# State-space output products in pairs of banks with the latents' norms ahead of them, and split latent-attention scores, in a one-core Trainium2 block kernel

## What is computed

```python
z = x @ w_in                      # x: layer-normed input
xs, gs, cq, ckv, kr, gm = split(z)
# state-space branch, 32 groups of 16 channels, 64 complex states
y = einsum(c_re, h_re) - einsum(c_im, h_im) + d_skip * xs
y = gelu(y);  y = y * sigmoid(y @ w_glu + b_glu)
# latent attention, 4 heads, 128 + 64 rotary dimensions
q  = rms_norm(cq) @ w_uq;   kv = rms_norm(ckv) @ w_ukv
s  = (q_nope @ k_nope.T + rot(q_rope) @ rot(k_rope).T) * scale   # causal
o  = softmax(s) @ v
mix = concat(ys * silu(gs), o * silu(gm)) @ w_out
u   = ALPHA * x + mix
```

## Time and profile before

| | us |
|---|---|
| median of 3 runs (2264.51 to 2267.73) | 2265.94 |
| the profiled execution's own time | 2264.39 |
| its span, first to last instruction | 2262.4 |
| TensorE busy / ACT / DVE / POOL | 2186.6 / 753.0 / 1163.2 / 1190.1 |
| mean granted TensorE clock | 0.991 |

### The profile page before, as it was taken

One profiled execution on the slowest core, in us unless ns is written; L12 is line 12 of the kernel. 1 busy time (PEld: TensorE's weight loads), 2 busy tenths in 40 slices (PEclk: granted clock), 3 DMA queues, 4 the chain that ended last, 5 costly groups with the idle time before them and its releaser, 6 DMA issues.

```text
span 2262.4 us, 27546 instructions
## 1 busy us (share of the span) xinstructions
PE 2186.6 (97%) x10904; PEld 1606.9 (71%) x10904; DVE 1163.2 (51%) x1479; ACT 753.0 (33%) x1163; POOL 1190.1 (53%) x808
## 2 busy tenths in 40 slices
PE   8999999999998999999999999998999999999998
PEld 3445563677886786568866788876788888888886
DVE  6960752553186612540047624775866666652424
ACT  5111133231112502650045343135454445532211
POOL 2443420206796464435746764374688888844441
PEclk9999999999999999999999999999999999999999
DMA  5334323003221421101212235233122222144112
GB/s 227 103 93 89 82 64 110 15 1 121 96 100 61 153 75 66 43 1 40 91 21 61 77 110 214 102 112 131 47 84 83 80 79 81 66 170 158 47 38 75
DMA packets 63134, 196.12 MB, mean 87 GB/s; under 512 B 14935, under 2 KB 17287, under 8 KB 62447
## 3 DMA queue, kind: packets, MB, share of 16 engines
q1 hardware_dynamic: 52048, 148.54, 19.8%
q10 hardware_dynamic: 7888, 32.26, 3.7%
q0 software_dynamic: 3072, 13.58, 2.7%
HBM read 154.34 MB, written 37.78 MB: 85 GB/s over the span
## 4 chain that ended last, share of the span: by engine, by line
PE 89%; DVE 4%; ACT 3%; issue 2%; POOL 1%; DMA 0%; DVEq 0%; ACTq 0%; SPq 0%
PE ps L3100 21%; PE ps L2758 16%; PE ps L2723 13%; PE ps L3219 11%; PE ps L3024 4%; PE ps L3133 3%; PE ps L327 3%; PE ps L3171 2%; PE ps L493 1%; PE ps L481 1%; PE ps L350 1%; PE ps L997 1%; PE ps L2838 1%; PE ps L618 1%; PE ps L630 1%
## 5 line engine op out<-in xcount | busy, mean ns | idle before, releaser
L1498 POOL TENSOR_TENSOR w_parts<-front,sb_zero 128x1024 fp32r<-128x1024 f32 x69 | 140.5, 2037 | 374.5 <-PE ps L3219 117.7
L3219 PE MATMUL ps<-ffn_parts,w_parts 128*128 128x512 f32 x1008 | 230.3, 389 | 1.5 <-DVE front L2684 1.5
L1573 POOL TENSOR_TENSOR up_parts<-front,up_parts 128x512 fp32r<-128x512 f32 x120 | 194.5, 1627 | 69.5 <-ACT up_parts L1841 69.4
L2723 PE MATMUL ps<-front 128*128 128x512 f32 x512 | 223.8, 595 | 0.0
L1503 POOL TENSOR_TENSOR w_parts<-front,w_parts 128x1024 fp32r<-128x1024 f32 x75 | 208.8, 2784 | 22.9 <-ACT w_parts L1996 7.5
L3219 PEld LDWEIGHTS ps<-ffn_parts,w_parts 128*128 128x128 f32 x1008 | 189.0, 188 | 41.7 <-issue 2.6
L1411 POOL TENSOR_TENSOR front<-front,sb_csilu 128x1024 f32<-128x1024 f32 x48 | 102.7, 2140 | 216.9 <-DMA front<-w_ada 216.9
L3100 PE MATMUL ps<-t_high,up_parts 128*128 128x512 f32 x640 | 204.8, 391 | 5.0 <-ACT back L1848 5.0
L2758 PE MATMUL ps<-h_high,w_parts 128*128 128x512 f32 x672 | 187.6, 394 | 0.6 <-PE ps L3024 0.6
L2723 PEld LDWEIGHTS ps<-front 128*128 128x128 f32 x512 | 96.0, 190 | 114.7 <-issue 114.7
L3100 PE MATMUL ps<-h_high,up_parts 128*128 128x512 f32 x480 | 154.5, 389 | 1.5 <-DVE back L2452 1.5
(11 more groups left out here) (406 smaller groups left out, 4552.5 us busy)
## 6 DMA issues: line engine op xcount, KB each, us to landing
front<-w_ada SPq DMA_DIRECT2D x48, 512.0 KB, 3.6
front<-w_up SPq DMA_DIRECT2D x44, 512.0 KB, 4.2
front<-w_down SPq DMA_DIRECT2D x22, 512.0 KB, 3.5
front<-w_in SPq DMA_DIRECT2D x16, 512.0 KB, 3.5
front<-w_out SPq DMA_DIRECT2D x16, 512.0 KB, 4.4
residual<-back ACTq DMA_DIRECT2D x2, 4096.0 KB, 14.9
front<-w_gates SPq DMA_DIRECT2D x16, 512.0 KB, 4.0
gates<-back SPq DMA_DIRECT2D x16, 512.0 KB, 3.1
```

What stands on the lines that cost most here:

```text
L1498: pool.tensor_tensor(high, raw, zero[:, 0:1].to_broadcast((P, PAGE)), ALU.add)\
L1573: pool.tensor_tensor(parts[:, BANK:], src, parts[:, 0:BANK].bitcast(F32), ALU.subtract)\
L2723: mm = pe.matmul(ps[:, bank + nt, :], ring[:, slot, at + k * step:at + k * step + P], rhs(k0 + k)[:, nt * BANK:(nt + 1) * BANK], start=sta ...
L3219: mm = pe.matmul(ps[:, 2 * m + nt, :], parts[n % 2 + w_][:, at:at + P], half_of(AR[kk % 4 + x_], nt), start=k == 0 and q == 0, stop=k == N ...
```

## The change

The state-space output is made in four rounds r instead of eight steps: two banks are open at once (5 and 6, or 2 and 3), first the eight 128-row products, then sixteen 64-row products that alternate between rows 0 to 63 (one bank) and rows 64 to 127 (the other). The norms' squares, sums, roots, reciprocals, spreads and scales are moved to earlier places in each stream. Keys, queries and rotary parts are kept as high and low parts; scores are five fp32r products over 128 rows. The low parts of keys and queries lie where XN was, so XN is written to DRAM after the embedding norm and read back by POOL after the attention. Some semaphores are merged (`ONE_COUNT`, `T`), which leaves the waits as they are.

```diff
 latent_sums_pe: one buffer, sums of ckv in columns 0:256 and of cq in 256:512 of bank 7
 latent_spread_pe(pe, N):
-    for j in range(4):
-        mm = pe.matmul(ps[:, j, 0:256], pick[at, :], ...)
+    for j in (0, 2, 1, 3):           # LATENT is now the halves of banks 5 and 6
+        if j == 1:
+            mm.then_inc(S("half_spread"), 1)
+            pe.wait_ge(S("half_spread"), 2 if N == "q_norm" else 1)
+        mm = pe.matmul(LATENT[:, j, :], pick[at, :], LATENT_ROOT[N][at, :], ...)
 mla_items:
+    wide = 256 if qb == 0 else 768 if qb == 4 else w
-    sc.append((c0, c1, QN[:, h, q], KN[:, h, c0:c1], True, False))
-    sc.append((c0, c1, QR[:, h, q], KROT[:, c0:c1], False, True))
+    sc.append((c0, c1, QNH[h][:, q], KNH[h][:, c0:c1], True, False))
+    sc.append((c0, c1, QNH[h][:, q], KNL[h][:, c0:c1], False, False))
+    sc.append((c0, c1, QNL[h][:, q], KNH[h][:, c0:c1], False, False))
+    sc.append((c0, c1, QRS[h][:, q], KRH[:, c0:c1], False, False))
+    sc.append((c0, c1, QRS[h][:, q], KRL[:, c0:c1], False, True))
 POOL:
-    pool.wait_ge(S("norm_ready"), tiles_to("q_norm", 2))
+    pool.wait_ge(S("dve_step"), DVE_STEP["cm_zero"])     # ahead of the four loads of kr
     pool.wait_ge(S("mla_turned"), 32)
+    pool.dma_start(XN, xn_dram).then_inc(S("xn_back"), 16)
 ACT:
     embed_act(act)
+    act.wait_ge(S("norm_ready"), tiles_to("ln_emb", FT))
+    act.dma_start(xn_dram, XN).then_inc(S("xn_in_dram"), 16)
     z tile 10:  + latent_square_act(act, 0)
     x == 16:    + latent_square_act(act, 1)
     x == 20:    + latent_square_act(act, 2)
     after x = 23:
+    latent_root_act(act, "kv_norm", 2);  latent_root_act(act, "q_norm", 2)
     z tile 14:  + latent_gain_act(act, 0)
     z tile 15:  + latent_gain_act(act, 1), (act, 2)
     x == 27:    + the two Sin of the rotary tables (were before x = 24)
 DVE:
     dve.wait_ge(S("ssm_ps_read"), 24)
+    latent_rstd_dve(dve, "kv_norm")
     ...
     dve.wait_ge(S("scanned"), 2 * PAIRS)
+    latent_rstd_dve(dve, "q_norm");  latent_dve(dve, "kv_norm", (0,))
     ...
     dve.sem_inc(S("dve_step"), 1)                        # states_ready
+    latent_dve(dve, "q_norm", (1, 2))
     ...
-    link(dve.memset(QR, 0.0))
+    for m in range(4):
+        dve.wait_ge(*T("kv_free", m + 1))
+        dve.tensor_tensor(KNL[m], two(2 * (m % 2)), KNH[m].bitcast(F32), ALU.subtract).then_inc(S("k_low"), 1)
     rotary part of the keys, then KRH = copy, KRL = subtract
+    the same for QNL, then_inc(S("q_low"), 1)
     rotary parts of the queries: multiply, multiply, add, then per head copy and subtract of 64 rows
     before u:   + dve.wait_ge(S("xn_back"), 16)
 TensorE:
     after tile 11:  + latent_sums_pe(pe, 0)
     after x == 19:  + latent_sums_pe(pe, 1)
     after x == 23:  + latent_sums_pe(pe, 2)
     after tile 13:  + latent_spread_pe(pe, "kv_norm")
     after tile 14:  + latent_spread_pe(pe, "q_norm")
-    for x in range(24, 32): ...
+    pe.wait_ge(S("norm_scaled"), tiles_to("q_norm", 2))
+    for r in range(4):
+        if r == 1:
+            pe.wait_ge(S("z_free"), 16)
+        elif r >= 2:
+            pe.wait_ge(S("ssm_ps_read"), 22 + 2 * r)
+        for j in range(4):
+            for odd in range(2):
+                pe.matmul(state(j, odd), TM[:, g, :], UU[:, g, :], start=j == 0, stop=False)
+        for j in range(4):
+            for i in range(2):
+                for odd in range(2):
+                    pe.matmul(state(j, odd), CP[h, i, q, GC:GC + P], SS[h, i, q, :], ...)
     keys:    m == 1 waits for ssm_ps_read 32;  m >= 2 waits for k_low m - 1 too
     values:  kt == 0 waits for k_low 4 too
     queries: m >= 2 waits for q_low m - 1 too;  the rotary tiles wait for q_low 4 too
```

More of the change, by code:

```diff
@@ L1091, in embed_dve @@
                     .then_inc(S("norm_scaled"), 1)
[L1093 removed]
+        TEMPS_2 = (cols(48 * PAGE + 512, 49 * PAGE + 512),)
+        LATENT_ROOT = {N: cols(49 * PAGE + 512 + 256 * i, 49 * PAGE + 768 + 256 * i)
+                       for i, N in enumerate(("kv_norm", "q_norm"))}
+        STATE_BANK = (5, 6, 2, 3)
         TEMPS_3 = (page(12), page(13), page(14))
@@ L1660, in _ @@
                 z(tile, CQ[:, tile - 8, :] if tile < 10 else (CKV if tile == 10 else KR), ACT.Copy)
+                if tile == 10:
+                    act.wait_ge(S("dve_step"), DVE_STEP["g_skip"])
+                    act.wait_ge(S("z_free"), 11)
+                    latent_square_act(act, 0)
             act.wait_ge(S("u_landed"), 16 * STEP)
@@ L1670, in _ @@
                 z(tile, GM[:, tile - 12, :], ACT.Silu)
[L1672 to L1677, removed]
+                if tile == 14:
+                    latent_gain_act(act, 0)
+            latent_gain_act(act, 1)
+            latent_gain_act(act, 2)
             for x in range(24, 32):
@@ L1703, in _ @@
             for m in range(4):
-                act.wait_ge(S("q_tile"), m + 1)
-                act.activation(QN[:, m, :], two(2 * (m % 2)), ACT.Copy).then_inc(S("q_free"), 1)
+                act.wait_ge(*T("q_tile", m + 1))
+                act.activation(QNH[m], two(2 * (m % 2)), ACT.Copy).then_inc(S("q_free"), 1)
             act.wait_ge(S("yf_landed"), 16)
@@ new lines, in _ @@
+            tt(page(47), page(47), SIN, ALU.mult)
+            tt(page(46), page(46), page(47), ALU.add)
+            link(dve.tensor_copy(KRH, page(46)))
+            tt(KRL, page(46), KRH.bitcast(F32), ALU.subtract)
+            for m in range(4):
+                dve.wait_ge(*T("q_free", m + 1))
+                dve.tensor_tensor(QNL[m], two(2 * (m % 2)), QNH[m].bitcast(F32), ALU.subtract).then_inc(S("q_low"), 1)
+            for m in range(2):
+                dve.wait_ge(*T("qr_tile", m + 1))
+                tt(page(47), two(4 * m), COS, ALU.mult)
+                tt(page(22), two(4 * m + 2), SIN, ALU.mult)
+                dve.sem_inc(S("qr_free"), 1)
+                tt(page(47), page(47), page(22), ALU.add)
+                for i in range(2):
+                    own, other = slice(64 * i, 64 * i + 64), slice(64 - 64 * i, 128 - 64 * i)
+                    link(dve.tensor_copy(QRS[2 * m + i][own, :], page(47)[own, :]))
+                    tt(QRS[2 * m + i][other, :], page(47)[own, :], QRS[2 * m + i][own, :].bitcast(F32), ALU.subtract)
@@ L2849, in _, with state @@
-            pe.wait_ge(S("norm_scaled"), tiles_to("q_norm", 2))
+            pe.wait_ge(S("norm_scaled"), tiles_to("q_norm", 2))
[4 more added lines that the diff above has]
+                    pe.wait_ge(S("ssm_ps_read"), 22 + 2 * r)
+                def state(j, odd):
+                    return ps[:, STATE_BANK[2 * (r % 2) + odd], j * P:(j + 1) * P]
+                for j in range(4):
+                    for odd in range(2):
+                        g = 8 * r + 2 * j + odd
+                        mm = pe.matmul(state(j, odd), TM[:, g, :], UU[:, g, :], start=j == 0, stop=False,
+                                       skip_group_check=True)
+                        if r == 0 and j == 0 and odd == 0:
+                            mm.then_inc(S("w_used"), 1)
+                for j in range(4):
+                    for i in range(2):
+                        for odd in range(2):
+                            h, q = slice(64 * odd, 64 * odd + 64), 4 * r + j
+                            mm = pe.matmul(state(j, odd), CP[h, i, q, GC:GC + P], SS[h, i, q, :], start=False,
+                                           stop=j == 3 and i == 1, skip_group_check=True)
+                            if j == 3 and i == 1:
+                                mm.then_inc(S("ssm_ps"), 1)
```

169 lines of the change are left out of this document (84 added, 85 removed).

## The result

| | before | after |
|---|---|---|
| median of runs, us | 2266.73 (2264.51 to 2267.73, 4 runs) | 2244.12 (2242.8 to 2246.37, 4 runs) |
| ratio | 1 | 0.9903, 95% interval 0.9888 to 0.9917 |
| the profiled execution: own time / span / mean granted clock | 2264.39 / 2262.4 / 0.991 | 2246.37 / 2244.4 / 0.987 |

Faster by 22.6 us in medians, where 26.1 was forecast. The forecast, 2239.8, is 4.3 too low; 0.8 of that is the median of before, which stands at 2266.73 here and at 2265.94 in the forecast. The range holds the result. The profiled execution of after lies 2.25 above its median and that of before under its own, so the two profiles are only 18.0 apart.

A forecast was written before the change was run, and what follows sets the result against it. TensorE was taken as the bound, 89% of the chain of waits. Terms -18.0 + 2.3 + 4.4 - 15.75 + 0.7 = -26.35, with handovers -26.1, gave a median of 2239.8 us, range 2230 to 2251.

The forecast's parts named there:

- State products: State-space output: four rounds with fewer shape changes and overlapping array halves take 15.9 instead of 33.9 us, -18.0.
- rival 1: State-space rounds: array halves do not overlap at 128 columns, +7.2, so 2247; chance 0.12.
- Norms ahead: Before the state-space rounds: split spreads add 0.8 and ACT's squares 1.5, DVE's work stays covered; +2.3 us.
- Low parts: Keys and queries: TensorE waits longer for DVE's low parts, +2.65 at keys to values, +1.8 at rotary tiles; +4.4 us.
- Attention: Latent attention: fp32r scores at one cycle a column cut a middle head from 29.26 to 25.1 us; -15.75 in all.
- (4): Attention scores: fp32r records of 256 columns only run at the float32 rate, +24.6, so 2264, no change; chance 0.04.
- (5): Attention scores: fp32r records of 384 columns too run at the float32 rate, +43.6, so 2283, slower; chance 0.05.
- XN: Output projection: issuing XN's read on POOL delays the second tile, +0.7 us; the read's landing stays hidden.
- Numbers: Closing part: range 2230 to 2251, lower-clock stretches shifting 2 or 3 us either way; faster 0.91, same 0.04, slower 0.05.
- (2): Attention: the DVE-ACT chain becomes the bound and half of the 15.75 turns into idle time, 2247.5; chance 0.11.
- (3): Output projection: XN's read collides with `projected` and the weights, third tile or POOL waits 5 to 8, 2246; chance 0.07.

The follow-up runs named there:

- Experiment 5: Changed kernel with the old order within a round, each group's 128-row products then its 64-row ones: 2262.16 us, ratio 0.9985.
- experiment 2: Changed kernel with each round's 64-row products reordered, all of rows 0 to 63 first, then all of rows 64 to 127: 2249.28 us, ratio 0.9923.
- experiment 1: Changed kernel with the scores back as two float32 products of the former width, low parts still made: 2257.65 us, ratio 0.996.
- experiment 4: Changed kernel with unread products in TensorE's waits ahead of key tile 2, the values and the rotary tiles: 2241.92 us, ratio 0.9895.
- experiment 9: Changed kernel with XN read back on ACT's queue instead of POOL's, nothing else: 2241.79 us, ratio 0.9902.
- 11: Repeat, side by side, of the changed kernel (2243.92 us) and the same with unread products in its new waits (2242.65 us).
- 10: Changed kernel with values between keys, rotary tiles and gate in other banks, XN on ACT's queue, kr loads still first: 2233.75 us, ratio 0.9858.
- experiment 3: Changed kernel without widening the first and fifth query blocks' scores, so some records have 128 columns: 2244.28 us, ratio 0.9903.
- experiment 8: Changed kernel with values between keys, rotary tiles in free banks, XN on ACT's queue, eight writes ahead of kr loads: 2250.94 us, ratio 0.9934.

## Why the prediction was right, and where it missed

**State products, -18.0: right.** The stage went from 33.9 of products to 15.67, where 15.9 was forecast. Experiment 5 gives the 18.0 back. The parts are right as well: 0.056 a record in pairs where 0.057 was taken, 0.112 in one half alone, 0.19 to 0.20 a change of shape. The overlap that rival 1 doubted is worth the 7.2 that it was priced at, 4 x 16 x 0.112; experiment 2 takes away 5.8 of it. A small slip in the working: the four sums and spreads that it names add up to 2.85, not 2.7.

**Norms ahead, +2.3: about 0.8 too low.** The first round starts at 303.16, where 302.3 was expected. The three sums and two split spreads take 3 x 0.57 + 2 x 1.40 = 4.5 on TensorE, where 3.5 (2.7 + 0.8) was counted; ACT's squares cost 1.2, where 1.5 was counted. TensorE did not wait for DVE ahead of the round: cover held, and by more than the 1.2 counted, since DVE's last scale ended at 297.6 where 301.1 was summed.

**Low parts, +4.4: the waits right, their consequence missed.** Keys to values 10.73 against 11.1, the wait ahead of the rotary tiles 2.45 against 3.0. The term came to 3.6 (2.3 for the keys, 1.3 for the queries), because a low part of keys or queries takes 1.24, where the 1.48 of another subtraction was taken as undisturbed. That one is slower by no property of its form: the low part of the rotary keys reads SBUF as it does and takes 1.23. POOL works on its own tiles beside the four of the earlier trace rows and not beside this one; whether that is the reason no run shows. But the steps behind the waits grew by 1.5 (9.39 against 7.87 for the values) and 1.7 (15.98 against 14.28), at a clock of 0.83 and 0.89. The gate therefore ends 8.25 earlier than before (399.71 against 407.95), not 11.3.

**Attention, -15.75: right in size, 1.6 of it hidden by the clock.** Middle heads 25.08 and 25.12, forecast 25.1; whole stretch 116.3 to 102.6 in the profiled executions, -13.75, but 116.53 (experiment 1) to 100.98 (experiment 4), -15.55, where both are at full clock, and -15.3 from before's own 116.3. Narrow records at one cycle a column were the right end of the bounds for 256 columns and up: rivals 4 and 5 needed 0.43 for 256 columns and the trace has 0.12. That no smaller width saves anything would not have changed the sum, since the change has none.

**XN, +0.7: right.** POOL's issue takes 0.57, the split ends 18.19 after its start where it was 17.58. The 4 MB landed in 14.5 in place of the 20 I took, and `projected` in 20.0 instead: the second read waited, not the first. Nothing waited for either.

**What was mis-sized** is a sentence under "Numbers": "The stretches at lower clock lie later and may fall otherwise, 2 or 3 us in either direction". It was a symmetric allowance for stretches that exist, and it put at nothing what half clock can cost behind the new and longer waits that the change gives TensorE. In the profiled execution such stretches cost 1.5 at the values, 1.7 at the first rotary tile, 1.6 in the first head (102.57 against 100.98), 1.5 in the projection's tile (7.32 against 5.78) and 1.8 later (one stretch of 10.2 instead of 6.8), 8.2 in all. The rest came to -26.2, where -26.35 was summed: the products and norms fell 0.6 short, the attention 0.4, and the low parts cost 0.8 less. That these cancel is luck. -26.2 + 8.2 is the -18.0 measured between the two profiles. In the medians less of it shows, because executions differ in which stretches they have: -22.6 against -26.1.

Shown: the value and rotary steps are slow by the clock alone (4, 9, 11). Not shown, though likely: that the waits bring the stretches, and that filling or removing them keeps the clock up. Both profiles with filled waits have the two steps at full clock, and with the waits gone no stretch comes before 682 (10), but experiment 9 has none before 687 with all its waits in place. Open: what decides in which execution a wait is followed by one.

**Rivals.** (1) fell by the pairs in the changed profile and by experiment 2. (2) would have shown TensorE idle more than about 1.2 a head; it is idle 0.8 in 25.08. (3) fell: nothing waited for XN. (4) and (5) fell by the single records.

## What to carry to other kernels

Group products by their shape in the array: each change between 128 and 64 rows cost 0.2 us here, and halves alternated product by product ran at 0.056 a record instead of 0.112. When a change lengthens what TensorE waits for before it may reuse a bank, price the wait and the half clock that can follow it (1.5 to 1.7 us each here), and look for independent tiles and free banks to put there: this took 8 us more off (10 against 9), by an order and by banks alone. Before moving small loads behind large writes on a queue, ask who waits for the loads.

## What the runs showed of the hardware that was not expected

- Two products over different halves of the array's rows start within 0.01 us of each other, and the pair takes the time of one: 0.112 for two records of 128 columns (the changed kernel's rounds), against 0.112 for each in one half (experiment 2).
- fp32r records of 128 rows follow each other every 0.11 at 128 columns (experiment 3) and every 0.11 to 0.12 at 256, 0.17 to 0.18 at 384 and 0.23 at 512: going from 256 columns to 128 saves next to nothing.
- Waits of TensorE of 1.9 to 2.5 us were followed by 3.4 us at the lower of the two clock levels (1.2 GHz of 2.4) in some executions and not in others of the same kernel (the changed kernel's two profiles, experiment 9). With unread products in two of the waits the level stayed at 2.4 GHz there in both profiles, and fell at later waits in one of them.
- Inside a wait of 14.67 us the level fell too, and it stayed down for 17.1 us in all (experiment 8).
- 256 KB loads on POOL's queue behind eight writes of 256 KB landed up to 20.80 us after their issue (experiment 8).
